# Feed-forward of a hybrid decoder layer: the first two down-projection tiles of each part interleaved, the convolution-state transposes placed behind them

## The reference

```python
def conv_ffn(h, buf, w_up, cw, cb, w_dn):
    t = h.shape[1]
    u = h @ w_up                                    # 2048 -> 2 * 5632
    full = jnp.concatenate([buf.astype(u.dtype), u], axis=1)
    c = cb
    for j in range(CONV_W):                         # causal depthwise convolution, width 3
        c = c + full[:, j:j + t] * cw[j]
    a, gt = jnp.split(c, 2, axis=-1)
    out = (jax.nn.gelu(gt, approximate=True) * a) @ w_dn   # 5632 -> 2048
    return out, full[:, t:]
```

## Time and profile before

| | |
|---|---|
| median of 3 runs | 2157.35 us (2153.27 to 2161.8) |
| profiled execution | 2164.7 us |
| its span | 2163.2 us |
| TensorE busy | 2051.2 us, 95% of the span |
| VectorE busy | 1067.9 us, 49% |
| ScalarE busy | 881.0 us, 41% |
| mean granted TensorE clock | 0.954 |
| HBM traffic | 151 GB/s over the span |

### The profile page before, as it was taken

How to read it: one execution, slowest core, us unless ns; L and a number is a source line. 1 busy time by engine, 2 the same in 40 slices (tenths; PEclk the granted TensorE clock), 3 DMA queues, 4 the chain that set the end, 5 groups by cost and what they waited for, 6 DMA issues and landing times. The chain is left out here.

```text
span 2163.2 us, 35972 instructions
## 1 busy us (share of the span) xinstructions
PE 2051.2 (95%) x14038; PEld 1997.4 (92%) x14038; DVE 1067.9 (49%) x1621; ACT 881.0 (41%) x1332; POOL 104.2 (5%) x156
## 2 busy tenths in 40 slices
PE   6999899999799999899997999999999999999897
PEld 4998898999699999899995999999999999999895
DVE  4332354222256767455336655543555543455455
ACT  5322455322234444344234554432444442344443
POOL 0000020222000000010000000000000000000000
PEclk9998599988799999999998999999999999999997
DMA  7664653555546565467752455555555555555452
GB/s 211 178 182 144 177 142 105 152 152 158 167 120 168 144 164 140 133 194 197 182 152 78 118 155 150 142 153 144 148 155 146 145 150 144 154 153 142 121 140 89
DMA packets 535236, 323.99 MB, mean 150 GB/s; under 512 B 7841, under 2 KB 522322, under 8 KB 534392
## 3 DMA queue, kind: packets, MB, share of 16 engines
q1 hardware_dynamic: 518848, 272.12, 46.4%
q0 software_dynamic: 11024, 44.96, 6.7%
q10 hardware_dynamic: 5288, 5.86, 0.8%
HBM read 304.93 MB, written 22.04 MB: 151 GB/s over the span
## 5 line engine op out<-in xcount | busy, mean ns | idle before, releaser
L994 DVE TENSOR_TENSOR wlo<-raw,whi 128x2048 fp32r<-128x2048 f32 x261 | 598.3, 2292 | 865.5 <-ACT whi L570 865.5
L1430 PE MATMUL ps<-hH,whi 128*128 128x320 f32 x2752 | 867.1, 315 | 12.2 <-DVE hL L1014 5.0
L1430 PE MATMUL ps<-hL,whi 128*128 128x320 f32 x2752 | 856.6, 311 | 0.0
L1430 PE MATMUL ps<-hH,wlo 128*128 128x320 f32 x2752 | 856.2, 311 | 0.0
L570 ACT ACTIVATE whi<-raw 128x2048 fp32r<-128x2048 f32 x261 | 499.4, 1913 | 758.5 <-PE ps L1430 619.1
L1430 PEld LDWEIGHTS ps<-hH,whi 128*128 128x128 f32 x2752 | 522.8, 190 | 19.9 <-issue 11.8
L1430 PEld LDWEIGHTS ps<-hL,whi 128*128 128x128 f32 x2752 | 522.9, 190 | 0.2
L1430 PEld LDWEIGHTS ps<-hH,wlo 128*128 128x128 f32 x2752 | 522.3, 190 | 0.0
L1430 PE MATMUL ps<-aH,whi 128*128 128x320 f32 x704 | 218.4, 310 | 2.6 <-DVE aL L1374 2.6
L1430 PE MATMUL ps<-aL,whi 128*128 128x320 f32 x704 | 217.9, 309 | 0.0
L1430 PE MATMUL ps<-aH,wlo 128*128 128x320 f32 x704 | 217.9, 309 | 0.0
(11 more groups left out here) (280 smaller groups left out, 1846.4 us busy)
## 6 DMA issues: line engine op xcount, KB each, us to landing
raw<-in_w_up SPq DMA_DIRECT2D x88, 1024.0 KB, 5.7
raw<-in_w_in SPq DMA_DIRECT2D x85, 1024.0 KB, 5.5
raw<-in_w_down SPq DMA_DIRECT2D x32, 1024.0 KB, 5.9
raw<-in_w_out SPq DMA_DIRECT2D x16, 1024.0 KB, 5.9
raw<-in_w_down SPq DMA_DIRECT2D x16, 768.0 KB, 5.0
raw<-in_w_branch_a SPq DMA_DIRECT2D x16, 512.0 KB, 4.1
raw<-in_w_branch_b SPq DMA_DIRECT2D x16, 512.0 KB, 5.4
merge_gates<-mgate ACTq DMA_DIRECT2D x32, 160.0 KB, 1.9
```

Of the source, the lines that this page charges most:

```text
L994: TT(wlo[:, slot], raw[:, slot], whi[:, slot].bitcast(F32), ALU.subtract).then_inc(lo_ready, 1)
L1430: ins = pe.matmul(out, ww[:, slot, w, :], xx[:, k, :], start=(start and q == 0 and p_ == 0), stop=(stop and q == last and p_ == 2), skip_g ...
```

## The change

Three things are edited. TensorE: a new function `first_two` takes the place of the first turn of the down loop in each part. It issues all blocks of the first tile but the last, then the first `lead` blocks of the second tile (3 where the part has 16 blocks, 7 where it has 12), then, after the wait for `a_lo` at `i0`, the last block of the first tile, and the rest of the second. TensorE, last part: the 18 transposes are issued behind these two tiles. ScalarE: the copies to `crow_out` are made in the first turn of the down loop of the last part, between the second tile's split and its square. The later turns of the down loop are as before. The number of instructions is the same.

```diff
--- before.py
+++ after.py
@@ -947,12 +947,14 @@
 
                     turns(act, KT // 2, turn)
                 else:
-                    for i in range(5):
-                        w = 4 if i < 4 else 2
-                        act.wait_ge(nc_ps, i + 1)
-                        act.activation(crow_out[:, 4 * i:4 * i + w, :],
-                                       ps[0:2 * FT, 3 + i, 0:w * P].rearrange("p (a d) -> p a d", a=w), ACT.Copy
-                                       ).then_inc(nc_ok, 1)
+                    def conv_rows():
+                        for i in range(5):
+                            w = 4 if i < 4 else 2
+                            act.wait_ge(nc_ps, i + 1)
+                            act.activation(crow_out[:, 4 * i:4 * i + w, :],
+                                           ps[0:2 * FT, 3 + i, 0:w * P].rearrange("p (a d) -> p a d", a=w), ACT.Copy
+                                           ).then_inc(nc_ok, 1)
+
                     act.wait_ge(x_add, KT)
 
                     def square(m, u, j):
@@ -965,6 +967,8 @@
                     def turn(j):
                         for u in range(2):
                             split_after(n0 + u, j, 2)
+                            if not later(j) and u == 1:
+                                conv_rows()
                             square(j * 2 + u, u, j)
 
                     turns(act, KT // 2 - 1, turn)
@@ -1807,25 +1811,33 @@
                 n0 += 2 * cnt
                 r0 += 2 * cnt
                 i0 += cnt
-                if part == 2:
-                    pe.wait_ge(hist_ok, 4)
+                tiles = [(k, k) for k in range(cnt)]
+
+                def first_two():
+                    lead = 3 if cnt == KT else 7
+                    pe.wait_ge(free[0], r0 // 2)
+                    pe.wait_ge(a_lo, i0 - 1)
+                    gemm(n0, n0 % 2, ps[:, 0, 0:T], aH, aL, tiles[:-1], done=False, stop=False)
+                    pe.wait_ge(free[1], r0 // 2)
+                    gemm(n0 + 1, (n0 + 1) % 2, ps[:, 1, 0:T], aH, aL, tiles[:lead], done=False, stop=False)
                     pe.wait_ge(a_lo, i0)
-                    for i in range(5):
-                        for q in range(4 * i, min(4 * i + 4, 2 * NSEQ)):
-                            ins = pe.transpose(ps[0:2 * FT, 3 + i, (q - 4 * i) * P:(q - 4 * i + 1) * P],
-                                               newc[:, :, q], ident)
-                        ins.then_inc(nc_ps, 1)
+                    gemm(n0, n0 % 2, ps[:, 0, 0:T], aH, aL, tiles[-1:], wait=False, start=False)
+                    gemm(n0 + 1, (n0 + 1) % 2, ps[:, 1, 0:T], aH, aL, tiles[lead:], wait=False, start=False)
+                    if part == 2:
+                        pe.wait_ge(hist_ok, 4)
+                        for i in range(5):
+                            for q in range(4 * i, min(4 * i + 4, 2 * NSEQ)):
+                                ins = pe.transpose(ps[0:2 * FT, 3 + i, (q - 4 * i) * P:(q - 4 * i + 1) * P],
+                                                   newc[:, :, q], ident)
+                            ins.then_inc(nc_ps, 1)
+
                 def turn(j):
+                    if not later(j):
+                        first_two()
+                        return
                     for u in range(2):
                         pe.wait_ge(free[u], j + r0 // 2)
-                        tiles = [(k, k) for k in range(cnt)]
-                        if not later(j) and u == 0:
-                            pe.wait_ge(a_lo, i0 - 1)
-                            gemm(n0, n0 % 2, ps[:, 0, 0:T], aH, aL, tiles[:-1], done=False, stop=False)
-                            pe.wait_ge(a_lo, i0)
-                            gemm(n0, n0 % 2, ps[:, 0, 0:T], aH, aL, tiles[-1:], wait=False, start=False)
-                        else:
-                            gemm(j * 2 + (n0 + u), (n0 + u) % 2, ps[:, u, 0:T], aH, aL, tiles)
+                        gemm(j * 2 + (n0 + u), (n0 + u) % 2, ps[:, u, 0:T], aH, aL, tiles)
 
                 turns(pe, KT // 2, turn)
                 n0 += KT
```

## The result

The changed kernel takes 2147.28 us, the median of 14 runs (2140.15 to 2152.32), against 2159.98 us for the kernel before on the same chips (14 runs). The ratio is 0.9944, with a 95% interval of 0.9930 to 0.9958: 0.56% faster. The profiled execution has a span of 2150.7 us against 2163.2, 12.5 us less.

What follows compares the result with a forecast made beforehand. TensorE was taken as the bound, with time won only at its stalls and half clock. 9.9 us in the last part plus 2.6 us in the first two made 12.5 us off the 2157.35 us median: 2145 us, range 2139 to 2153.

Steps and rivals of the forecast that it cites:

- TensorE is the bound, and time comes from its waits and its half clock: Whole change: TensorE bounds the kernel, so time is won only at its stalls or half clock; 12.5 us.
- Last part, D0 and D1: Last part's first two down tiles: interleaving leaves 0.25 us of the 8.0 us wait; 9.9 us saved in this part.
- D2's start: Start of the last part's third down tile: 2060.02 us before, 2050.12 after, with a new 0.45 us stall.
- Transposes: The 18 transposes behind the last part's first two tiles: 2.3 us at full clock, bounds 2.3 and 3.7 us.
- S: Time from the last up-projection matmul's start to the third down tile's start in the last part; 23.58 us before, 13.74 forecast.
- Copies on ScalarE: Five copies in the last part, 2.63 us: cost nothing, hidden in ScalarE's idle time; uncovered up to 2.6 us.
- Parts 0 and 1: First two parts of the down-projection: three blocks ahead of the wait save 1.32 us each, 2.6 us in both.
- Weights: Last part's weight loads beside the `crow_out` stores: cost taken as 0; 6.0 us if a load waited for all of the store.
- rival (b): Last part: a late load or late ScalarE turn costs 1 to 6 us, once, giving 2147.5 us; chance 0.12.
- One sign of being wrong that I named: Last part's later down tiles: standing over 5.3 us apart would show the forecast wrong.
- The clock, rival (a): Last part: the clock falls behind the transposes, costing 1.7 us; 10.8 us saved, 2146.5 us; chance 0.34.
- Slower, rival (d): Last part: stores keep each later weight load late; slower by 0.5% would be 2168 us; chance 0.04.

Runs made afterwards that it cites:

- the kernel with the first two parts alone: First two parts interleaved with a lead of 3 blocks, last part put back as in the kernel before: 2158.91 us, ratio 0.9986.
- the transposes twice: The changed kernel with the 18 transposes issued twice in the same place, 36 in all: 2140.16 us, one execution.

## Why the prediction was right

- *TensorE is the bound, and time comes from its waits and its half clock.* Right. From the second row on, the table of stretches comes down to these two and to the new waits.
- *Last part, D0 and D1.* D2's start in the kernel before, worked out from a split as 2060.02, is 2059.96 in the timeline, 0.06 us off. D0's last block was to start 8.31 us from the last up-projection matmul, and started at 8.24; the rest of the wait was 0.16 us for 0.25.
- *Transposes.* Sized at 2.3 us, they take 1.9, below the lower end of my bounds, because I spread the 1.04 us of eight of them over eight starts, the last one's own length included. It changed nothing: the wait behind them is 0.7 us instead of 0.45, and D2 is held by the chain. S was forecast at 13.74 and is 13.83; with `acc` ahead of the split it is 13.35, which shows that the chain through `acc` held D2, as was thought.
- *Copies on ScalarE.* Nothing, as said; 0.56 us of the cover are left.
- *Parts 0 and 1.* 2.64 forecast, 2.65 measured, three blocks being right and seven too many.
- *Weights.* The term I took as 0, and the only one of the sum that was clearly off. The stretch behind D2 grew by 1.01 us in the profiled execution and by 0.1 to 0.7 in the other kernels with the last part interleaved, where the clock stayed; 0.1 of it is D2's second matmul, the rest late loads. This is rival (b), and its price was low in its range of 1 to 6 us. The forecast and (b) thus both came true in part. Two causes, not one: the stores beside the loads, and D4's own load, which now has 5.9 us and sometimes needs more, it seems for an `instruction` packet beside it. I had taken the median load of 5.1 us, and not looked at the 6.0 us of the one load that matters. The 6.3 us worked out as the time a load has was close: D6's cost TensorE 0.2 us at 6.3, and 0.8 at 6.8. One sign of being wrong that I named did come: D5 to D6 are 5.99 us apart, and D2 to D3 and D4 to D5 5.38, over the 5.3 that I allowed.
- *The clock, rival (a).* It didn't happen: 1.00 in the profile after and in each kernel with the transposes in this place and the interleaving. With none in eight executions, my chance of 0.34 for it was too high. The Trainium skill, "TensorE: Matmul & The Clock Gate", Part 4: PE-mode transpose, says that a transpose doesn't count as activity in the way a matmul does. These runs don't bear it out, though the rows list the transposes as MATMUL and don't show whether that mode is on: 54 in a row left the clock at 1.00, and in the kernel with the first two parts alone it rose behind 18 at 0.50. What let it fall at 377 us no run here varied; the 2.06 us idle there, among few and small matmuls, is the likelier reason. The 48 transposes at the end, which I took from the earlier trace rows as a sign for the rule, are none: the clock rose while they ran in five of the thirteen profiled executions, one of which is shown above, though neither in the one before nor in the one after the change. What decides whether transposes raise it is open.
- *Slower, rival (d).* It didn't happen: the stores lengthened two loads, not eleven.

The sum was 12.5; the parts that belong to it came to 11.4 in the profiled execution, and the measured ratio gives 12.1 (9.1 to 15.1); the medians lie 12.7 apart. So the number fits better than its terms: in the profiled execution, 1.1 us of scatter ahead of the change made good what the loads took.

## What to carry to other kernels

Where an engine waits for the last result of a stage, work of the next tile can be put in front of the wait, but only as much as the tile after it can spare: count the chain that the interleaved tile has to cover (here 5.2 us from the first tile's last matmul to D2) and keep that many matmuls behind. Work that must be done somewhere is free in the shadow of such a chain, and transposes there do more than idle time does: the clock stayed in all eight profiled executions that have them there, and fell in one of two that have nothing. When a change takes slack out of a loop, look at the slowest transfer at that place, not at the median.

## What the runs showed of the hardware

- 18 to 54 transposes in a row, 1.9 to 5.8 us, left TensorE's clock at 1.00, and in one execution it rose from 0.50 to 1.00 behind 7.9 us of nothing and 18 transposes, 3.9 us. An empty stretch of 2.7 us let it fall in one execution, at a cost of 2.7 us, and not in another of the same kernel.
- A transpose of 88 columns of weights and 128 of data took 0.109 us at 1.00 and 0.213 at 0.50, from start to start.
- The same load of 768 KB at the same place took 5.0 to 6.6 us without stores beside it, over 5.4 us in just the eight executions of thirteen that had a 16 KB packet of the `instruction` queue within its first 3.3 us. With 704 KB of stores beside them, two others took 5.6 to 6.8 us instead of 5.0 to 5.2.
- The stages that no kernel here changes differ by up to 13 us between executions. One part is a wait of 13.4 us for `KTs` at 551 us in the changed kernel, behind a weight load for which ScalarE stood 17.9 us; with the transposes twice it was 8.5 us, behind 14.0. The four executions with 8.2 to 8.6 us here began the up-projection at 1169.7 to 1175.6 us, the nine with 12.3 to 13.4 at 1179.6 to 1182.7.
